# Two attentions in one fused float32 program: values in portions with zero-padded heads, and scores of stacked rows

## The chip, the cores and the metric

One core of one Trainium2 chip runs the whole program in one launch. The metric is the device time of that launch in microseconds (us). Below, TensorE is the matrix engine (its rows say PE, its weight loads PEld), VectorE is DVE, ScalarE is ACT, GpSimd is POOL, and SyncE (SP) issues most of the transfers.

## What is computed

A batch of one with 1024 tokens of width 1024 goes through a short-convolution layer, a stick-breaking attention layer, and a second block with two attentions of its own, a gated merge and a convolved FFN. Everything is float32. The parts that matter here:

```python
def stick_breaking_attention(q, k, v):        # 16 heads of 64
    ...
        z = jnp.einsum('bhqd,bhkd->bhqk', qb, kb) * inv_sqrt_d
    ...
        log_1m_beta = jnp.where(mask, log_beta - z, 0.0)
        suffix = lax.cumsum(log_1m_beta, axis=3, reverse=True) - log_1m_beta
        a = jnp.where(mask, jnp.exp(log_beta + suffix), 0.0)
        outs.append(jnp.einsum('bhqk,bhkd->bhqd', a.astype(vb.dtype), vb))
    ...
    o = o * jax.nn.silu(z)                     # z: the other half of h @ w_qz
    return x + gate[:, None, :] * (o @ w_out)

def _diff_attention(q, k, v, lam, lam_init, subln_g, slopes):   # 4 heads, 2 maps of 64
    ...
        p = jax.nn.softmax(scores, axis=-1)
        a = p[:, :, 0] - lam * p[:, :, 1]
        return jnp.einsum('bhqs,bshe->bqhe', a.astype(v.dtype), v)
    ...
    out = _rmsnorm(out, subln_g) * (1.0 - lam_init)
```

The other attention of the second block is a sliding window of 128 tokens: 8 heads of 64 over 2 key heads, with a sink.

## The kernel before, in words

The program is written out engine by engine; every engine runs its own list, and the lists meet in semaphores that are waited for by name (`at("stick_scan", n)` is the count after which scan n is done). The dense layers are a list of units, products of one 128-column weight tile with the whole activation (line 1362): both operands are split into a high and a low part (`w_hi`, `w_lo`; POOL makes them, lines 1212 and 1217) and three products are added, since TensorE takes its rounded float32 type faster. Each unit's result is read by an engine of its own. In the same way q and k of both attentions lie in DRAM as a high and a low part.

**First attention.** 128 items, one for each head and block of 128 queries, in the order of `STICK_ORDER` (blocks 6, 7, 0, 1, 4, 5, 2, 3 of each head). The steps of a loop over n hold work on different items. TensorE: scores of item n (`scores`, lines 561, 562, and a mask product at 564), the values of the item pair that ends at n - 6 (line 596, on every second step), the transposes of item n - 3 (`turn`, line 576). ScalarE: two sigmoids of the scores (783, 785), then the copies of the transposed block to `a_T` (797). VectorE: a scan over the sigmoid (908), which makes the suffix product. POOL: the factor times that (1264), giving `beta`, four buffers. The lags are the constants `TURN_LAG`, `VALUE_LAG`, `OUT_LAG`. Scores of an item may start when the scan of the former item of the same PSUM banks is done. The values of a head lie in `hin[:, s, 3]` as two packed parts, high and low, so the product's 128 output rows hold both halves of one head: the high part in the head's own 64 rows, the low part in the other 64. To add them, ScalarE copies one half to `s_o` (771), VectorE adds the other (899), and when both heads of a pair are there POOL multiplies by the gate `sz` (1246) and splits the result into `opA` (1250, 1253), the operand of the units of w_out. The value loads (line 1132) stand on SP's queue among the weight loads; `value_in` says when they are in. The parts of v are made behind the units of w_kv: TensorE transposes a unit's output, ScalarE copies it twice (1614), VectorE subtracts (2216), and `v_dram` takes both.

**Second attention.** 16 sliding-window steps (4 blocks of one head each) and then 32 differential steps, one for each head and query block, in the order `DIFF_ORDER` (0, 1, 2, 3, 7, 6, 5, 4). A differential step x has scores of map 1 and map 0 (line 655), VectorE's bias with running maximum (962), ScalarE's exp with sum (828), VectorE's combination of the two maps (997), the turn (675) at lag `DIFF_TURN`, the values (715) at lag `DIFF_VALUE`. Queries and keys have 64 rows a head, so each score is three products of 64 rows (q_hi k_hi, q_lo k_hi, q_hi k_lo), of map 1 on rows 64 to 127 and of map 0 on rows 0 to 63. Four items make a half of a head; behind its values ScalarE squares them, TensorE sums the squares with a product with ones (736), and adds eps times the squared sum of exps by four more products (738). Keys of a head (512 KB, two slots) and its values come in by SP (476, 491), and are waited for whole.

## Time and profile before

| what | value |
|---|---|
| median of 3 runs | 2885.86 us (2883.86 to 2886.23) |
| profiled execution, its own time | 2888.37 us |
| its span | 2886.6 us |
| TensorE busy | 2730.2 us (95%) |
| TensorE weight loads busy | 2273.4 us (79%) |
| VectorE busy | 1331.7 us (46%) |
| ScalarE busy | 876.1 us (30%) |
| POOL busy | 849.6 us (29%) |
| first attention, TensorE's first score product to its last value product | 937.38 to 1245.98 us |
| second attention, TensorE's first score product to its last product | 1725.56 to 1952.62 us |

A busy share is an average over stages with different limits: in the units TensorE is nearly alone, in the attentions four engines take turns in a ring. The span is that of the profiled execution, and the runs' times are of other executions of the same program.

### The profile page before, as it was taken

The page shows a single profiled execution, that of the slowest core. Times are in us where ns is not written, and L with a number is a line of the kernel's source. Part 1 is how long each engine was busy: PE and PEld are TensorE (multiplying, and loading weights), DVE is VectorE, ACT ScalarE, POOL GpSimd, SP SyncE. Part 2 cuts the span into 40 slices and gives each one's busy share as a digit, 9 for nine tenths or more (in the row PEclk, how much of TensorE's full clock was granted, in tenths as well). Part 3 has the DMA queues.
Part 4 walks back from the last instruction along what each step waited for, and adds up shares of the span by engine and source line. Part 5 has one row for each costly group of instructions (what it writes and reads, how often), then busy time and mean ns, then how long its engine had stood idle before and what let it go on. Part 6 is the DMA issues. An engine that isn't in the chain of part 4 may idle for free.

```text
span 2886.6 us, 33895 instructions
## 1 busy us (share of the span) xinstructions
PE 2730.2 (95%) x13015; PEld 2273.4 (79%) x13015; DVE 1331.7 (46%) x1758; ACT 876.1 (30%) x1521; POOL 849.6 (29%) x600
## 2 busy tenths in 40 slices
PE   3899999999899899999999999898999999999998
PEld 2688888788778888877888878777878888888877
DVE  5656665631433666647300007763565423441444
ACT  3300012511411787846111017661252101110111
POOL 1133331022223566620332330113102233233235
PEclk7999999999999999999999999899999999999999
DMA  5244443263456444432443133103231111111113
GB/s 208 88 131 147 135 145 107 81 218 118 168 198 180 114 107 117 110 117 74 148 144 131 51 85 128 45 23 103 73 88 37 51 51 44 52 51 44 52 50 119
DMA packets 302013, 298.19 MB, mean 103 GB/s; under 512 B 15475, under 2 KB 247324, under 8 KB 300572
## 3 DMA queue, kind: packets, MB, share of 16 engines
q1 hardware_dynamic: 292092, 254.61, 29.6%
q10 hardware_dynamic: 9760, 41.42, 3.7%
q8 instruction: 103, 1.69, 0.3%
q14 instruction: 58, 0.48, 0.1%
HBM read 241.98 MB, written 54.00 MB: 103 GB/s over the span
## 4 chain that ended last, share of the span: by engine, by line
PE 80%; DVE 8%; ACT 4%; POOL 3%; DMA 3%; issue 2%; SPq 0%; DVEq 0%; ACTq 0%; POOLq 0%
PE PS L1362 61%; PE PS L1406 4%; PE PS L596 3%; PE PS L576 2%; PE PS L1429 1%; DMA mod_raw<-in_w_ada 1%; PE PS L655 1%; PE PS L715 1%; POOL beta L1264 1%; PE PS L1477 1%; DVE M L1909 1%; PE PS L675 1%; PE PS L637 1%; PE PS L561 1%; DVE w_lo L2009 1%
## 5 line engine op out<-in xcount | busy, mean ns | idle before, releaser
L1362 PE MATMUL PS<-opA,w_hi 128*128 128x512 f32 x4544 | 1417.3, 392 | 20.7 <-POOL w_lo L1217 13.7
L1362 PEld LDWEIGHTS PS<-opA,w_hi 128*128 128x128 f32 x4544 | 858.8, 189 | 201.8 <-POOL w_lo L1217 14.7
L1362 PE MATMUL PS<-opA,w_lo 128*128 128x512 f32 x2272 | 888.6, 391 | 0.0
L1212 POOL CAST w_hi<-w_raw 128x1024 fp32r<-128x1024 f32 (+1 forms) x174 | 181.3, 1042 | 1585.5 <-PE PS L1362 1127.9
L1362 PEld LDWEIGHTS PS<-opA,w_lo 128*128 128x128 f32 x2272 | 429.6, 189 | 89.1 <-issue 0.2
L1217 POOL TENSOR_TENSOR w_lo<-w_raw,w_hi 128x1024 fp32r<-128x1024 f32 (+1 forms) x176 | 425.1, 2415 | 91.5 <-ACT w_hi L1697 77.6
L1362 PE MATMUL PS<-opB,w_hi 128*128 128x512 f32 x1216 | 379.8, 391 | 6.8 <-POOL w_lo L1217 4.4
L1362 PEld LDWEIGHTS PS<-opB,w_hi 128*128 128x128 f32 x1216 | 229.0, 188 | 55.9 <-POOL w_lo L1217 4.8
L1909 DVE SCALAR_TENSOR_TENSOR M<-mod_raw,small,M 128x512 f32<-128x512 f32 x168 | 170.0, 1012 | 171.2 <-DMA mod_raw<-in_w_ada 90.2
L1362 PE MATMUL PS<-opB,w_lo 128*128 128x512 f32 x608 | 237.1, 390 | 0.0
L2192 DVE SCALAR_TENSOR_TENSOR X<-PS,mod,X 128x512 f32<-128x512 f32 x96 | 72.1, 751 | 278.2 <-PE PS L1362 277.5
L908 DVE TENSOR_TENSOR_SCAN M<-PS,beta 128x896 f32<-128x896 f32 (+7 forms) x86 | 115.1, 1353 | 82.9 <-ACT PS L785 82.5
L2138 DVE TENSOR_SCALAR yt<-M,cols 128x512 f32<-128x512 f32 x44 | 65.2, 1482 | 163.4 <-ACT M L1849 160.4
L596 PE MATMUL PS<-a_T,hin 128*128 128x256 f32 (+1 forms) x640 | 139.7, 366 | 0.0
L929 DVE CUSTOM_DVE_ANT_0 prob<-bias,PS 128x256 f32<-128x256 f32 x64 | 23.1, 418 | 252.5 <-PE PS L637 252.5
L1849 ACT ACTIVATE M<-PS 128x512 f32<-128x512 f32 x44 | 26.4, 600 | 353.2 <-PE PS L1362 340.0
L1362 PEld LDWEIGHTS PS<-opB,w_lo 128*128 128x128 f32 x608 | 114.5, 188 | 24.0 <-issue 0.5
L596 PEld LDWEIGHTS PS<-a_T,hin 128*128 128x128 f32 x640 | 117.6, 192 | 15.1
L1264 POOL TENSOR_TENSOR beta<-beta,M 128x895 f32<-128x895 f32 (+7 forms) x86 | 103.1, 1209 | 68.5 <-ACT s_o L771 40.4
L797 ACT ACTIVATE a_T<-PS 128x512 f32<-128x512 f32 (+1 forms) x192 | 87.5, 492 | 52.4 <-PE PS L576 52.4
L2203 DVE SCALAR_TENSOR_TENSOR stage<-PS,stage 128x1024 fp32r<-128x1024 f32 x25 | 30.6, 1225 | 146.4 <-ACT stage L1776 145.9
L2143 DVE SCALAR_TENSOR_TENSOR yt<-M,cols,yt 128x511 f32<-128x511 f32 (+1 forms) x120 | 94.9, 790 | 4.2
(193 smaller groups left out, 3099.2 us busy)
## 6 DMA issues: line engine op xcount, KB each, us to landing
mod_raw<-in_w_ada SPq DMA_DIRECT2D x96, 256.0 KB, 3.0
w_raw<-in_w_up SPq DMA_DIRECT2D x44, 512.0 KB, 3.8
w_raw<-in_w_in SPq DMA_DIRECT2D x34, 512.0 KB, 3.8
w_raw<-in_a_w_in SPq DMA_DIRECT2D x32, 512.0 KB, 4.8
q_dram<-stage ACTq DMA_DIRECT2D x16, 1024.0 KB, 4.0
hin<-q_dram SPq DMA_DIRECT2D x64, 256.0 KB, 6.1
k_dram<-stage ACTq DMA_DIRECT2D x13, 1024.0 KB, 4.1
mod_raw<-in_b_mod_w SPq DMA_DIRECT2D x48, 256.0 KB, 2.9
```

Source lines behind the costliest of these rows:

```text
L596: ins = pe.matmul(dst, v, a_T[g % 2][:, kb, cols_of], start=(kb == 0), stop=(kb == i), skip_group_check=True)
L797: act.activation(dst, src, ACT.Copy).then_inc(act_done, 1)
L908: dve.tensor_tensor_scan(rest[n % FACTORS][:, 0:w][:, ::-1], stick_z(n)[:, ::-1], beta[n % BETAS][:, 0:w][:, ::-1], 1.0, ALU.mult, ALU.byp ...
L1212: pool.tensor_copy(hi, raw).then_inc(pool_done, 1)
L1217: pool.tensor_tensor(lo, raw, hi.bitcast(F32), ALU.subtract).then_inc(pool_done, 1)
L1264: pool.tensor_tensor(b[:, 0:w - 1], b[:, 0:w - 1], rest[n % FACTORS][:, 1:w], ALU.mult).then_inc(pool_done, 1)
L1362: ins = pe.matmul(ps, w[:, k0 + k, :], rhs(part, k0 + k), start=(k == 0 and n == 0), stop=(k == chunks - 1 and n == 2))
L1406: ins = pe.matmul(PS[:, bank(v, hf), :], weight(v, w, k), op_in[:, part, k, hf * HALF:(hf + 1) * HALF], start=(k == 0 and n == 0), stop=(k ...
L1909: dve.scalar_tensor_tensor(out=acc, in0=mod_raw[:, n % 2, :], scalar=c, in1=acc, op0=ALU.mult, op1=ALU.add).then_inc(dve_done, 1)
L2138: dve.tensor_scalar(o, src[:, t0:t0 + HALF], w_of(2), b, ALU.mult, ALU.add).then_inc(dve_done, 1)
L2143: dve.scalar_tensor_tensor(out=o[:, lo:], in0=src[:, t0 + lo - back:t0 + HALF - back], scalar=w_of(tap), in1=o[:, lo:], op0=ALU.mult, op1= ...
L2192: dve.scalar_tensor_tensor(out=X[:, j, t], in0=PS[:, bank(u, hf), :], scalar=mod[:, gate, j:j + 1], in1=X[:, j, t], op0=ALU.mult, op1=ALU. ...
```

## The change

First attention: v is stored once, unsplit (`vplain`), so one copy on ScalarE and no subtraction. Each head's values are loaded to a tile `head_v` of 128 columns per key block of which the other head's 64 are zero (cleared once by POOL). The two heads of a pair then add into the same PSUM banks and rows of their own, and one product by `sz` on VectorE a half is all that is left; ScalarE's copy, VectorE's add and POOL's product by `sz` go. The values of an item pair stand in two portions on two successive steps, `a_T` has four slots, `beta` five, and the lags are 4, 7 and 9.

Second attention: q_hi stands over q_lo in the 128 rows of `opA[:, e, c]`; k_hi is loaded twice, to rows 0 to 63 and 64 to 127, and so is k_lo. Two products of 128 rows make a score, now with q_lo k_lo too. Keys come by map and by halves of 512 columns into three slots. Turn, value and square lags are 2, 4 and 3, pair and probability buffers three, and eps times the squared sum is added to the squares by POOL (`square_eps`) in place of the four products. At the first item of a head the scores of map 0 stand behind the turn.

```diff
-TURN_LAG, VALUE_LAG, OUT_LAG = 3, 6, 7
-BETAS, FACTORS = 4, 3
+TURN_LAG, VALUE_LAG, OUT_LAG = 4, 7, 9
+BETAS, FACTORS = 5, 3
...
-DIFF_TURN, DIFF_VALUE, RMS_LAG = 3, 5, 2
+DIFF_TURN, DIFF_VALUE, RMS_LAG = 2, 4, 3
...
-PAIRS = 4
+PAIRS, PROBS = 3, 3
...
+def key_slot(q):
+
+    return (0, 2, 1)[q % 3]
...
+def diff_map(q):
+
+    return q // 2, 1 - q % 2
...
+        beta = [at(f"beta{i}", AT_X + (28 if i == 4 else 4 * i) * KIB, [T]) for i in range(BETAS)]
+        a_T = [[at("a_T0", AT_M + 18 * KIB, [2, 2 * P])], [at("a_T1", AT_M, [4, 2 * P])],
+               [at("a_T2", AT_A + 28 * KIB, [4, 2 * P]), at("a_T2b", AT_A + 60 * KIB, [2, 2 * P])],
+               [at("a_T3", AT_X + 16 * KIB, [4, 2 * P]), at("a_T3b", AT_X + 20 * KIB, [4, 2 * P])]]
+        head_v = [at(f"head_v{i}", AT_B + (44 + 16 * i) * KIB, [T]) for i in range(2)]
...
         def second_loads(sp):
...
+            def dup(slot, hf, rows, name, cols_of):
+
                 for part in range(2):
...
+                    for place in range(2):
+                        sp.dma_start(keys[slot][part][place * DH:(place + 1) * DH, cols_of].bitcast(F32),
+                                     k2_dram[part, rows, cols_of]).then_inc(k_in[slot][hf], 16)
+                        step(k_in[slot][hf], *name, by=16)
+
+            def diff_keys(q):
+                j, m = diff_map(q)
+                slot = key_slot(q)
...
+                elif q < 3:
+                    sp.wait_ge(pe_done, at("sec_S", 4 * q + 7, 0))
...
+                    former, fm = diff_map(q - 3)
+                    sp.wait_ge(pe_done, at("sec_S", SWA_STEPS + NT * former + NT - 1, fm))
+                rows = slice((1 + j) * P + m * DH, (1 + j) * P + m * DH + DH)
+                for hf in range(2):
+                    dup(slot, hf, rows, ("k_in", "diff", q, hf), slice(hf * HALF, (hf + 1) * HALF))
...
+            diff_keys(1)
+            diff_keys(0)
+            diff_value(0)
+            diff_keys(2)
+            for j in range(1, DIFF_HEADS):
+                diff_value(j)
+                diff_keys(2 * j + 1)
+                if j < DIFF_HEADS - 1:
+                    diff_keys(2 * j + 2)
```

```diff
-            def values(n):
+            def values(n, part):
 
                 h, i = stick_item(n)
-                s, o, g = h % 2, 6 + i // NQ, n // 2
+                s, o = h % 2, 6 + i // NQ
...
+                middle = (i + 1) // 2 - (i > NQ)
+
+                if part == 0:
+                    if n % NT == 1:
+                        pe.wait_ge(value_in[s], at("value_in", h))
+                    if n == 1:
+                        pe.wait_ge(pool_done, at("head_zero"))
+                    pe.wait_ge(act_done, at("stick_hi", STICK_PLACE[n, i // NQ]))
+                    if h >= 2 and h % 2 == 0 and i in (1, NT - 1):
+                        pe.wait_ge(dve_done, at("stick_o", h // 2 - 1, i // NQ))
+                for kb in range(i + 1)[slice(middle, None) if part else slice(0, middle)]:
                     cols_of = slice(P if kb == i else 0, 2 * P)
-                    dst = PS[:, o, q0 + cols_of.start:q0 + 2 * P]
-                    v = hin[:, s, 3, kb * P:(kb + 1) * P].bitcast(F32)
-                    ins = pe.matmul(dst, v, a_T[g % 2][:, kb, cols_of], start=(kb == 0), stop=(kb == i),
+                    ins = pe.matmul(PS[:, o, q0 + cols_of.start:q0 + 2 * P], head_v[s][:, kb * P:(kb + 1) * P],
+                                    a_T[i // 2][kb // NQ][:, kb % NQ, cols_of],
+                                    start=(h % 2 == 0 and i in (1, NT - 1) and kb == 0), stop=(h % 2 == 1 and kb == i),
                                     skip_group_check=True)
-                ins.then_inc(pe_done, 1)
-                step(pe_done, "stick_v", n)
+                if part:
+                    ins.then_inc(pe_done, 1)
+                    step(pe_done, "stick_v", n)
 
...
-                if n >= VALUE_LAG and (n - VALUE_LAG) % 2:
-                    values(n - VALUE_LAG)
+                if n > VALUE_LAG:
+                    part = (n - VALUE_LAG) % 2 == 0
+                    values(n - VALUE_LAG - part, part)
                 if 0 <= n - TURN_LAG < STICK_ITEMS:
                     turn(n - TURN_LAG)
...
-                r = slice(DH * (n % 2), DH * (n % 2) + DH)
...
-                        for y, (pq, pk) in enumerate(((0, 0), (1, 0), (0, 1))):
-                            ins = pe.matmul(dst, opA[r, pq, n // 2, i * P:(i + 1) * P],
-                                            keys[r, n // 4, pk, k0:k0 + width], start=(y == 0), stop=(y == 2))
+                        for part in range(2):
+                            ins = pe.matmul(dst, opA[:, n % 2, n // 2, i * P:(i + 1) * P],
+                                            keys[n // 4][part][:, k0:k0 + width], start=(part == 0), stop=(part == 1))
                 ins.then_inc(pe_done, 1)
                 step(pe_done, "sec_S", x, 0)
...
+                if (x - SWA_STEPS) % NT in (0, NQ):
+                    pe.wait_ge(k_in[key_slot(q)][(x - SWA_STEPS) % NT // NQ], at("k_in", "diff", q, (x - SWA_STEPS) % NT // NQ))
...
-                    for y, (pq, pk) in enumerate(((0, 0), (1, 0), (0, 1))):
+                    for part in range(2):
                         ins = pe.matmul(PS[:, 2 * m + DIFF_BANK[x] + k0 // HALF, 0:width],
-                                        opA[r, pq, 4 + j, i * P:(i + 1) * P],
-                                        keys[r, j % 2, pk, k0:k0 + width], start=(y == 0), stop=(y == 2))
+                                        opA[:, m, 4 + j, i * P:(i + 1) * P],
+                                        keys[key_slot(q)][part][:, k0:k0 + width], start=(part == 0), stop=(part == 1))
...
-                pe.wait_ge(act_done, at("sec_sq", h))
-                pe.wait_ge(pool_done, at("sec_gd", items_of(h)[-1]))
-                pe.matmul(PS[:, turn_bank(c), :], ones[:], d_o[:, 0, :], start=True, stop=False, skip_group_check=True)
-                for b in range(NQ):
-                    ins = pe.matmul(PS[:, turn_bank(c), b * P:(b + 1) * P], eps_of[:], diff_diag[:, NQ * (h % 2) + b, :],
-                                    start=False, stop=True, skip_group_check=True)
-                ins.then_inc(pe_done, 1)
+                pe.wait_ge(pool_done, at("sec_sq_eps", h))
+                pe.matmul(PS[:, turn_bank(c), :], ones[:], d_o[:, 0, :], start=True, stop=True).then_inc(pe_done, 1)
                 step(pe_done, "sec_ss", h)
...
                     diff_scores(t, 1)
-                    diff_scores(t, 0)
+                    if (t - SWA_STEPS) % NT:
+                        diff_scores(t, 0)
...
+                if SWA_STEPS <= t < STEPS and (t - SWA_STEPS) % NT == 0:
+                    diff_scores(t, 0)
...
+            def finish(j, hf, n):
+
+                dve.wait_ge(pe_done, at("stick_v", n))
+                dve.wait_ge(reader(U_BOUT - 1), at("free", U_BOUT - 1))
+                if j:
+                    dve.wait_ge(pool_done, at("stick_out", j - 1, hf))
+                dve.tensor_tensor(s_o[:, hf, :], PS[:, 6 + hf, :], sz[:, j, hf * HALF:(hf + 1) * HALF],
+                                  ALU.mult).then_inc(dve_done, 1)
+                step(dve_done, "stick_o", j, hf)
```

```diff
+                sp.dma_start(head_v[s][:].rearrange(parts_of, b=NT, s=2)[:, :, s, :],
+                             v_dram[h // 2].rearrange(parts_of, b=NT, s=2)[:, :, s, :]).then_inc(value_in[h % 2], 16)
                 step(value_in[h % 2], "value_in", h, by=16)
 
...
+                def square_eps(h):
+
+                    pool.wait_ge(act_done, at("sec_sq", h))
+                    pool.wait_ge(pool_done, now(pool_done))
+                    pool.tensor_tensor(d_o[:, 0, :].rearrange("p (b q) -> p b q", b=NQ),
+                                       d_o[:, 0, :].rearrange("p (b q) -> p b q", b=NQ),
+                                       diff_diag[:, NQ * (h % 2):NQ * (h % 2) + NQ, :], ALU.add).then_inc(pool_done, 1)
+                    step(pool_done, "sec_sq_eps", h)
 
                 def low(h):
```

The first attention on TensorE, head 1, its items 8 to 10 and what stands around them (`hin` holds q and k, `beta` the items' products, `a_T` their transposes, numbers are buffers). Before:

```order
L576 MATMUL PS<-ident,beta_84 128x128 x5
L561 MATMUL PS<-hin 128x512
L562 MATMUL PS<-hin 128x512
L561 MATMUL PS<-hin 128x384
L562 MATMUL PS<-hin 128x384
L564 MATMUL PS<-mask_r,ident_r 128x128
L576 MATMUL PS<-ident,beta_85 128x128 x6
```

and now:

```order
L623 MATMUL PS<-a_T_92,head_v_95 128x256 x3
L601 MATMUL PS<-ident,beta_85 128x128 x5
L586 MATMUL PS<-hin 128x512
L587 MATMUL PS<-hin 128x512
L586 MATMUL PS<-hin 128x512
L587 MATMUL PS<-hin 128x512
L589 MATMUL PS<-mask_r,ident_r 128x128
L623 MATMUL PS<-a_T_92,head_v_95 128x256
L623 MATMUL PS<-a_T3b,head_v_95 128x256 x3
L623 MATMUL PS<-a_T3b,head_v_95 128x128
L601 MATMUL PS<-ident,beta_86 128x128 x6
```

The turns of an item stand one step further from its scores, and each step now has a portion of value products, where they stood in one block on every second step.

The differential steps on TensorE, end of the first half of a head (`aT` are transposes, `vals` values, `prob` exps, `keys` keys). Before:

```order
L675 MATMUL PS<-ident,prob_101 128x128 x7
L655 MATMUL PS<-keys,opA 128x256 x6
L715 MATMUL PS<-aT,vals_98 128x128 x8
L675 MATMUL PS<-ident,prob_103 128x128 x6
L655 MATMUL PS<-keys,opA 128x384 x6
L715 MATMUL PS<-aT,vals_98 128x128 x7
L736 MATMUL PS<-d_o,ones 128x512
L738 MATMUL PS<-diff_diag,eps_of 128x128 x4
L675 MATMUL PS<-ident,vals_97 128x128 x5
L655 MATMUL PS<-keys,opA 128x512 x6
```

and now:

```order
L706 MATMUL PS<-ident,prob_114 128x128 x5
L686 MATMUL PS<-keys_101,opA 128x384
L686 MATMUL PS<-keys_102,opA 128x384
L686 MATMUL PS<-keys_105,opA 128x384
L686 MATMUL PS<-keys_106,opA 128x384
L746 MATMUL PS<-aT,vals_107 128x128 x6
L766 MATMUL PS<-d_o,ones 128x512
L706 MATMUL PS<-ident,prob_115 128x128
L686 MATMUL PS<-keys_101,opA 128x512
L686 MATMUL PS<-keys_102,opA 128x512
```

Six score products of a piece of 512 or fewer keys are four, one product is left of the squares' five, and it stands one item later.

## Rows read from the trace of the kernel before

**Rows 1.** The page, chain that ended last, by engine

```profile
PE 80%; DVE 8%; ACT 4%; POOL 3%; DMA 3%; issue 2%; SPq 0%; DVEq 0%; ACTq 0%; POOLq 0%
```

**Rows 2.** Windows: length, busy us of each engine (instructions), granted clock, DMA share, GB/s

```profile
960.40:1224.70 264.30, 246.14 (x1512) 219.86 (x1512) 165.92 (x141) 213.53 (x421) 174.35 (x153) 0.99 0.43 110
...
1725.50:1744.50 19.00, 18.28 (x84) 17.36 (x84) 11.10 (x54) 11.08 (x40) 0.00 (x0) 0.51 1.03 300
1744.50:1803.00 58.50, 56.35 (x453) 52.02 (x452) 42.54 (x186) 43.57 (x141) 2.14 (x2) 1.00 0.25 89
1803.00:1940.40 137.40, 123.62 (x766) 100.33 (x766) 98.17 (x243) 88.37 (x202) 24.84 (x37) 0.89 0.08 28
```

**Rows 3.** Waits of PE, 960 to 1225: us in total, times, longest

```profile
PE PS L561 <- DVE M L908: 9.3, 10, 0.9
PE PS L561 <- DVE rest L908: 4.7, 5, 0.9
PE PS L576 <- POOL beta L1264: 4.6, 6, 0.8
```

**Rows 4.** Waits of DVE, 1744.5 to 1803

```profile
DVE prob L929 <- PE PS L637: 8.6, 7, 3.2
DVE opA L1004 <- ACT opA L846: 6.0, 6, 1.2
```

**Rows 5.** Waits of DVE, 1803 to 1940.4

```profile
DVE vals L962 <- PE PS L655: 14.7, 7, 3.1
DVE prob L962 <- PE PS L655: 10.3, 14, 2.7
```

**Rows 6.** Groups, 937 to 1250: form, count, busy us, mean ns, idle before

```profile
L1246 POOL TENSOR_TENSOR s_o<-s_o,sz 128x512 f32<-128x512 f32 x16 | 20.5, 1282 | 5.1 <-DVE s_o L899 5.1
...
L771 ACT ACTIVATE s_o<-PS 64x512 f32<-64x512 f32 x32 | 18.9, 592 | 3.4 <-PE PS L596 2.7
```

**Rows 7.** Timeline of PE: start, us, instructions, count (the same twelve products twice)

```profile
1112.21 4.28 PE L596 MATMUL PS<-a_T,hin 128*128 128x256 f32 x12
...
1132.25 2.59 PE L596 MATMUL PS<-a_T,hin 128*128 128x256 f32 x12
```

**Rows 8.** Timeline of PE behind the first attention; in brackets the idle time before

```profile
1252.94 0.50 PE L1362 MATMUL PS<-opA,w_hi 128*128 128x512 f32 x1 [1.91 <-POOL opA L1253]
```

**Rows 9.** Timeline at the first unit of w_qz

```profile
740.03 1.02 ACT L1599 ACTIVATE vt<-PS 128x1024 f32<-128x1024 f32 x1
...
741.31 0.77 PE L1429 MATMUL PS<-opA,w_hi 128*128 128x512 f32 x1 [5.00 <-DVE opA L1988]
```

**Rows 10.** DMA issues: count, KB each, median us to landing

```profile
hin<-v_dram SPq DMA_DIRECT2D x16, 512.0 KB, 4.3
...
vals<-va_dram SPq DMA_DIRECT2D x4, 256.0 KB, 8.6
```

**Rows 11.** Timeline of PE, start of the second attention

```profile
1725.56 8.91 PE L637 MATMUL PS<-keys,opA 64*128 64x128 f32 x42 [7.15 <-DMA opA<-q_dram]
```

**Rows 12.** Timeline of PE in a differential step, and a piece of the chain (units)

```profile
1879.69 0.97 PE L655 MATMUL PS<-keys,opA 64*128 64x512 f32 x6
1880.59 1.60 PE L715 MATMUL PS<-aT,vals 128*128 128x128 f32 x12
...
1699.83 18.60 PE PS L1362 x82
```

**Rows 13.** Timeline, end of the second attention

```profile
1938.80 0.89 DVE L997 SCALAR_TENSOR_TENSOR vals<-vals,small,vals 128x640 f32<-128x640 f32 x1
...
1951.57 1.05 PE L738 MATMUL PS<-diff_diag,eps_of 128*128 128x128 f32 x8
1960.38 0.79 PE L1362 MATMUL PS<-opA,w_hi 128*128 128x512 f32 x1 [7.75 <-POOL w_lo L1217]
```

**Rows 14.** Windows of 3 us: one in the first head, two behind the attention

```profile
1824.00:1827.00 3.00, 3.00 (x12) 2.50 (x12) 2.24 (x6) 1.51 (x3) 0.90 (x1) 0.50 0.00 0
...
1963.00:1966.00 3.00, 3.00 (x8) 2.32 (x8) 0.00 (x0) 0.00 (x0) 0.98 (x1) 0.50 0.97 321
1966.00:1969.00 3.00, 3.00 (x14) 2.43 (x13) 0.00 (x0) 0.00 (x0) 0.00 (x0) 0.99 0.98 335
```

246 lines of the change are left out of this document (88 added, 158 removed).

## The prediction, made before the changed kernel ran

> **What bounds the kernel now.** I read the profile's page first. Its chain is 80% TensorE [rows 1], so a microsecond taken from the other engines is worth something only where TensorE waits for it. The change touches two attentions. Only there, and at the seams around them, can time move; the unit products (line 1362) are untouched. So I cut the trace into windows [rows 2]. The first attention holds TensorE from 937.38 us (its first score product) to 1245.98; its even middle, fourteen heads, is the 264.3 us window, in which TensorE is busy 246.14 at a granted clock of 0.99. The second attention is two stretches: sixteen sliding-window steps (58.5 us) and the differential steps (137.4 us, TensorE busy 123.62, clock 0.89).
>
> In the first attention's middle TensorE waits 18.6 us in all: score products for the scan (9.3 + 4.7) and turns for the beta product on POOL (4.6) [rows 3]. These are one thing: with a short item next, the ring of score, two sigmoids, scan, beta product, turn comes round too late. ScalarE is in that ring and is 81% busy (213.53 of 264.3).
>
> In the second attention I read VectorE's waits, since scores, running maximum, exp and turn form a ring there too. In the sliding-window part VectorE waits for score products 8.6 us, 3.2 of it once at the start [rows 4]. In the differential part it waits for them 14.7 + 10.3 = 25.0 us [rows 5]. So neither TensorE nor VectorE is full there: each idles while the other holds the ring.
>
> **First attention, part by part.** *Removed:* ScalarE's half-output copies, 32 of 592 ns = 18.9 us, and POOL's products by sz, 16 of 1282 ns = 20.5 us [rows 6]. VectorE's 32 adds become 16 products by sz of 512 columns, half as many. Turn, value and output lags go from 3, 6, 7 to 4, 7, 9 steps with a fifth beta buffer, and the value products of an item pair come in two portions on two successive steps, where they now stand in one block of up to 16 (2.59 us for 12 [rows 7]). *Not changed:* the number of products. Values still take one 128x256 product per key block. So TensorE's busy 246.14 stays, and the gain can come from waits alone. A turn a step later has one more step of TensorE work (about 2.2 us, 264.3 / 112 items = 2.36 less the waits) to hide the scan and beta product; the longest wait of the 21 is 0.9. ScalarE has 18.9 us less to do in the ring. I take all 18.6 as gone. The 12 value products at 1112.21 took 4.28 us where the same twelve took 2.59 twenty us later [rows 7]: the clock fell once, after two waits of 0.93 and 0.78. With no waits I take that 1.7 as gone. **A: -20.3.** Bounds: 0 and -20.3, and I come near the far end because the cover (2.2 us) is over twice the longest wait.
>
> *Start.* Turns begin one step later and values too, and TensorE has less to do meanwhile, and the last items drain one step longer. One step costs 2.36 at most and 0 at least: **B: +2**. *Seam to w_out of that layer.* After the attention TensorE stops 1.91 us for POOL's second opA split [rows 8]; POOL's product by sz (1282 ns) ahead of it is gone and the whole is shorter: **C: -1.9**; bounds 0 and -1.9.
>
> *Seam between w_kv and w_qz.* VectorE's value split (two subtracts per value block) goes, and ScalarE's two copies become one. TensorE waits 5.00 us until 741.31, and ScalarE's value copy from PSUM still stands at 740.03 to 741.05 [rows 9]. That copy is not removed, only two of 1.31 before it become one, so the start moves little. **D: -1** with the smaller stalls behind. Bounds 0 and -2.
>
> *Value loads.* Per head 256 KB in runs of 64 numbers instead of 512 KB in long ones. The nearest rows are the sliding-window values, the same pattern at 8.6 us to landing, against 4.3 for today's value loads [rows 10]. It is issued when the values of the head before last are done and is wanted about a head (18.9 us, 264.3 / 14) later. Cost 0, hidden by that head; without that cover it would be 4.3 a head. The memsets of the zero columns stand in POOL's idle stretch before 937.
>
> **Second attention.** *Start.* The first 42 sliding-window score products take 8.91 us, 0.212 each, at half clock [rows 11]. Three products of 64 rows become two of 128, so 28: 14 x 0.212 = 3.0. The queries now come as 64-row pieces and I have no row for these, so I keep only **E: -1.8**; bounds 0 and -3.0. *Sliding-window steps.* Of the 8.6 us of waits [rows 4], the 3.2 at the start belongs to E's low clock. Of the other 5.4 I take 3.3, about three fifths: beside them VectorE waits 6.0 for ScalarE's output [rows 4], which the change leaves alone, and the steps bound there stay as they are. **F: -3.3**; bounds 0 and -5.4.
>
> *Differential steps.* Here the change says "two products instead of three", and the rows say otherwise. Six 64-row products of 512 columns, three on rows 0 to 63 and three on rows 64 to 127, run from 1879.69 to the next product at 1880.59: 0.90 us, 0.15 each. A full 128-row product of 512 columns costs 18.60 / 82 = 0.227 [rows 12]; four are 0.91. So on items up to 512 keys the two products cost what the three did. The Trainium skill, TensorEngine Tiling (Array Packing), section Tiling Modes, says of this that tiles on different rows work independently, with a speedup of up to 2, so that the change gives something up: by the full factor six products would cost 0.68 where four stacked ones cost 0.91, 36 such groups in the four heads would lose 8 us, and the sum would be -36. The trace bears out a factor of 1.5 (0.15 against 0.227), by which the two forms tie.
>
> What is gained is elsewhere: the four eps products behind each half's sum of squares go (8 records, 1.05 us [rows 13]; eight halves: 8.4 us of TensorE), the turn comes a step sooner, and only each head's key half that is needed is waited for. POOL adds one 128x512 sum per half (1282 ns by the same form in [rows 6]); the lag of the root-mean-square goes from two to three steps and covers it. Of the 25.0 us I keep half as still there: at head ends one item's scores must wait for values, turn and squares in TensorE's own order, four or five waits of nearly 3 (the longest is 3.1), and the clock is half for a stretch after 1819 [rows 14]. Keys: the load of each head's second map now waits for the last item of the map three back, and lands 4.3 to 8.6 us later (the two rows of [rows 10]); TensorE has one step of 4.3 us (137.4 / 32) plus that step's first scores and turns to do, and the second map's scores are put behind the turns for that. I cost it at nothing; without cover it is up to 2 a head at three heads. **G: -13**; bounds 0 and -25. *Last head.* From the last combine, at 1939.69, to the first branch product at 1960.38 is 20.7 us [rows 13]. A value lag one shorter, no eps products and earlier turns leave about 16: turn 0.6, values 2.6, squares' sum and its copy, then the same chain to w_lo. **H: -4.7**; bounds 0 and -8.
>
> **Sum.** -20.3 + 2 - 1.9 - 1 - 1.8 - 3.3 - 13 - 4.7 = **-44.0**. The profiled execution took 2888.37 us (span 2886.6), 2.5 above the median of 2885.86; so the changed one is 2844.4 profiled, and 2842 as a median.
>
> **Rivals.**
> *B1: the first attention keeps its waits.* ScalarE is 81% busy and its order changes; the fifth beta buffer may bring nothing if the scan itself is the bound (VectorE 165.92 of 264.3 speaks against it). Then A gives 5 rather than 20.3: -28.7, 2857 us. 0.10.
> *C1: the second attention gives nothing.* A shorter turn lag takes cover away: scores, maximum, exp and combination must be through within two steps, not three, and with three pairs of buffers rather than four VectorE waits for the turns of three steps ago, with that item's maximum and the combination behind it in its queue and ScalarE's exp behind those. Then E to H fall away: -44 + 22.8 = -21.2, **2865 us**. 0.10.
> *D1: the clock comes back sooner.* After the gap behind this attention, where the next products are of 128 rows, it was at half from the start at 1960.38 until 1966 only (0.50, then 0.99 [rows 14]), against the 19 us from 1725.5 (0.51 [rows 2]) with products of 64 rows. If stacked products do the same, 13 us fewer at half clock at the start and some 10 in the first head: the ratio of the two rows of [rows 7] is 1.65, so each gives back 0.4: 23 x 0.4 = 9 to 11, total about -55, 2831 us. 0.12.
> *E1: slower, by the clock.* The clock stays at its lower level through the whole second attention, since the ring's gaps now fall differently. The differential part's clock of 0.89 means about 30 of its 137.4 us at half; its TensorE work at full clock is then 123.62 - 30 + 30 / 1.65 = 112, less 8.4 for eps = 103, times 1.65 = 171: +33. The sliding-window steps: 56.35 less 54 products of about 0.13 = 49, times 1.65 = 81: +22. With E to H gone and A to D kept: -21.2 + 55 = **+34, 2920 us**. It makes the whole slower once about 40% of the second attention stands at low clock (21.2 / 55). Against it: in [rows 2] the clock came back each time, and the stacked products fill all rows. 0.05.
> That the change doesn't do what it says I see at one place only, the three-to-two products above, and the sum has it.
>
> **How the numbers follow.** Forecast 0.60 at 2842, B1 0.10, C1 0.10, D1 0.12, E1 0.05, and 0.03 for B1 and C1 together (-6, about no change). Upward the range takes in B1 and C1: 2866. Downward D1's 2831 and then G at its bound of -25 instead of -13, of which I take 11: 2820. **2820 to 2866**; E1, the joint case and the ends of the forecast are outside. A measurement can tell about 0.2%, 5.8 us. Slower by more: E1, 0.05. Within it: the joint case, 0.03. Faster: the rest, 0.92.
>
> **What would show it.** In the first attention: no waits of L561's line on the scan, and a distance of 17.5 to 17.9 us between heads in place of 18.9; clock 1.00. The add and the copies gone from ScalarE, whose busy falls by about 19. In the second: VectorE's waits for score products about 12 us in place of 25.0, and score products of 512 columns at 0.227, in pairs, with no saving of time per narrow item; the last combine to first branch product about 16 us. The prediction is wrong if the first attention still takes over 300 us, or if the second attention shows less than 10 us gained by its windows, or if the granted clock there lies under 0.8.

## The result and the profile after

| | before | changed |
|---|---|---|
| median | 2884.86 us (4 runs, 2880.42 to 2886.23) | 2833.49 us (4 runs, 2832.38 to 2836.87) |
| ratio, with 95% interval | | 0.9827 [0.9809, 0.9844] |
| span of the profiled execution | 2886.6 us | 2830.6 us |
| forecast | | 2842 us, range 2820 to 2866 |

The kernel is 51.4 us faster, 7.4 more than the -44.0 of the sum. Cut at the same places, the two profiled executions (2886.6 - 2830.6 = 56.0) say where. Every number of the table is a difference of starts on TensorE's timeline; the last combine is VectorE's, by its end. (The 1245.98 us given above as the end of before's first attention is the start of the first product of the units behind it, as in the table.)

| stretch | before | changed | difference | terms of the sum |
|---|---|---|---|---|
| start to the first transpose of v | 659.06 | 652.68 | -6.4 | none |
| to the first score product of the first attention | 278.32 | 277.94 | -0.4 | D -1 |
| first attention to the first product of the units behind it | 308.60 | 280.72 | -27.9 | A, B -18.3 |
| of it fourteen heads | 264.26 | 238.27 | -26.0 | A -20.3 |
| to the second attention | 479.58 | 477.86 | -1.7 | C -1.9 |
| its start to the first differential score | 74.40 | 64.72 | -9.7 | E, F -5.1 |
| to the end of the last combine (the differential steps) | 139.73 | 128.14 | -11.6 | G -13 |
| to the first branch product (the drain) | 20.69 | 21.06 | +0.4 | H -4.7 |
| to the end | 926.22 | 927.48 | +1.3 | none |

The first line is not the change's. In the fourteen kernels profiled for this study, on which TensorE has the same instructions in the opening, the second modulation sum (a group of small products with `ones`) starts anywhere from 136.98 to 142.24 us, and the sum after it from 184.07 to 190.89; before is at the late end (190.56), the changed kernel at the early one (184.16). So some 50 of the 56 are the change's, which is what the medians say.

The same fourteen show how closely the other lines can be read, since many of them share the instructions of a stretch. From the first transpose to the first attention takes 271.5 to 278.3 us, and from the first attention to the second 476.7 to 479.9, with and without the change, so D and C are not read from these two lines. Six kernels (the changed one, e2, e5, e6, e9, e11) have the changed second attention to the instruction: 64.7 to 65.2 us up to the first differential score, and 128.1 to 130.3 in the differential steps, where the changed kernel is the lowest. The three with the former one (before, e1, e3) have 73.4 to 74.6 and 138.9 to 141.2. A difference of 1 us is read in neither stretch. The fourteen heads are steadier: the eight kernels that share them have 238.28 us each.

The page and the waits of TensorE, 930 to 1225 us, changed kernel (us in total, times, longest):

```profile
PE 84%; DVE 8%; ACT 3%; DMA 3%; issue 1%; POOL 1%; SPq 0%; DVEq 0%; ACTq 0%; POOLq 0%
```

```profile
PE PS L586 <- DVE M L923: 3.5, 2, 2.8
PE PS L586 <- POOL w_hi L1229: 1.3, 1, 1.3
PE PS L601 <- ACT a_T L814: 0.9, 1, 0.9
PE PS L586 <- DVE rest L923: 0.2, 1, 0.2
```

All of these are ahead of the fourteen heads, in the fill. TensorE is now 84% of the chain [rows 1], and the three rows of [rows 3] have no counterpart in the steady heads. The windows, in the form of [rows 2]: the fourteen heads, then the start of the second attention, the rest of its sliding-window steps, and the differential steps.

```profile
952.37:1190.64 238.27, 238.27 (x1515) 216.04 (x1513) 158.59 (x127) 203.85 (x392) 157.81 (x139) 1.00 0.47 108
...
1689.00:1701.00 12.00, 9.23 (x47) 8.58 (x48) 8.20 (x40) 6.64 (x25) 0.00 (x0) 0.68 1.12 223
1701.00:1754.00 53.00, 47.81 (x406) 45.70 (x404) 43.45 (x195) 43.94 (x145) 2.14 (x2) 1.00 0.74 170
1754.00:1882.00 128.00, 100.49 (x649) 84.58 (x647) 99.02 (x249) 90.64 (x212) 33.42 (x43) 0.97 0.20 59
```

In the first row TensorE is busy for the whole of the window at full clock: the first attention is now bound by TensorE alone. In the second attention the clock is back after some 12 us where it took 19 before, and is 0.97 in the differential steps in place of 0.89, while TensorE is busy 100.49 of 128 and VectorE 99.02: there the ring is the bound. VectorE's waits there, in the form of [rows 5], for scores and for turns:

```profile
DVE prob L977 <- PE PS L686: 5.3, 5, 1.7
DVE prob L977 <- PE PS L706: 2.7, 9, 1.3
DVE vals L977 <- PE PS L686: 2.6, 3, 1.2
...
DVE vals L977 <- PE PS L706: 2.4, 2, 2.2
```

Those for scores are 7.9 us in place of 25.0; those for turns are 5.1 where they were 0.5. ScalarE has 204 of 238 us to do in the first attention where it had 213.5 of 264.

### The profile page after: what moved, and what is told of

Its sections match the earlier page's. It is cut to its first block, busy times and chain, and to the rows that moved or that the text cites. A ratio compares the mean times of both kernels' runs of the same rounds, so it can differ in the third digit from the quotient of the medians.

```text
span 2830.6 us, 33366 instructions
## 1 busy us (share of the span) xinstructions
PE 2677.3 (95%) x12783; PEld 2235.0 (79%) x12783; DVE 1310.7 (46%) x1726; ACT 860.8 (30%) x1481; POOL 844.2 (30%) x594
## 4 chain that ended last, share of the span: by engine, by line
PE 84%; DVE 8%; ACT 3%; DMA 3%; issue 1%; POOL 1%; SPq 0%; DVEq 0%; ACTq 0%; POOLq 0%
PE PS L1393 63%; PE PS L623 5%; PE PS L1437 4%; PE PS L601 2%; PE PS L1460 2%; DMA mod_raw<-in_w_ada 1%; PE PS L587 1%; PE PS L586 1%; PE PS L1508 1%; DVE M L1923 1%; PE PS L746 1%; PE PS L706 1%; DVE w_lo L2021 1%; DVE prob L977 1%; PE PS L686 1%
## 5 line engine op out<-in xcount | busy, mean ns | idle before, releaser
L623 PE MATMUL PS<-a_T,head_v 128*128 128x256 f32 x448 | 116.7, 378 | 0.0
L1993 DVE TENSOR_TENSOR xn<-X,M 128x512 f32<-128x512 f32 x80 | 57.4, 717 | 86.0 <-PE PS L1393 81.5
L800 ACT ACTIVATE beta<-PS 128x896 f32<-128x896 f32 (+7 forms) x128 | 83.4, 652 | 22.1 <-PE PS L589 20.4
```

What stands on the lines that cost most here:

```text
L623: ins = pe.matmul(PS[:, o, q0 + cols_of.start:q0 + 2 * P], head_v[s][:, kb * P:(kb + 1) * P], a_T[i // 2][kb // NQ][:, kb % NQ, cols_of], ...
L800: act.activation(beta[n % BETAS][:, 0:w], z, ACT.Sigmoid).then_inc(act_done, 1)
```

## The experiments

They were measured in three groups, each with its own runs of the kernel before: e1 to e4 with a median of 2882.13 us, e5 to e8 with 2883.23, e9 to e12 with 2879.98. The changed kernel, 2833.49, was measured beside 2884.86. So medians of different groups can differ by some 5 us for no reason of the kernels, and where a difference is as small as that it is taken from the traces' stretches instead.

### The two parts alone

e1 has the constants `TURN_LAG` to `BETAS`, the value tiles, portions and finishes of the first attention; e2 has the rest of the diff.

```diff
 # e1
+TURN_LAG, VALUE_LAG, OUT_LAG = 4, 7, 9
+BETAS, FACTORS = 5, 3
 DIFF_TURN, DIFF_VALUE, RMS_LAG = 3, 5, 2
...
 # e2
 TURN_LAG, VALUE_LAG, OUT_LAG = 3, 6, 7
 BETAS, FACTORS = 4, 3
+DIFF_TURN, DIFF_VALUE, RMS_LAG = 2, 4, 3
+PAIRS, PROBS = 3, 3
```

> Only the first attention's part of the change. Theory 1 (the two parts act alone, each in its own window): the first attention, 308.6 us from its first score product to the first product of the units behind it, falls by 28.0 as in the changed kernel, and the seams around it by 2; the whole by about 30. Rival (part of the 51 us is chance in the first 140 us, where the changed kernel's profiled execution was already 6.3 us ahead without a changed instruction on TensorE): the time falls by 30 too, but the position at 140 us stands as in before. Forecast as the prediction had it: -21.

> Only the second attention's part. Theory 1: 9.7 us less up to the first differential score, 11.6 less in the differential steps, nothing at the drain: about -21 in all, so that e1 and e2 add up to the whole change. Rival (the parts interact, by the clock or by ScalarE): the sum of the two differs from the whole by more than 5 us.

e1: 2849.92 us, ratio 0.9896 [0.9873, 0.992], -32.2. e2: 2862.28 us, ratio 0.9936 [0.9915, 0.9957], -19.9. Together -52.1, the whole change -51.4: the parts act alone, as far as intervals of 6 to 7 us to either side can tell. In e1 the first attention takes 280.79 us and the second attention's stretches are those of before (74.59, 138.93, 20.70); in e2 the first takes 308.64 and the second's are the changed kernel's (65.16, 128.95, 21.06). The rival of e1 holds for the profiled executions: e1's second modulation sum starts at 140.43 and e2's at 142.24, like before's 140.65 and not like the changed kernel's 137.08.

### What took the first attention's waits away

e3 is the kernel before with one more step of turn lag and the fifth beta buffer:

```diff
-TURN_LAG, VALUE_LAG, OUT_LAG = 3, 6, 7
-BETAS, FACTORS = 4, 3
+TURN_LAG, VALUE_LAG, OUT_LAG = 4, 6, 7
+BETAS, FACTORS = 5, 3
```

> The kernel before with a turn lag of 4 in place of 3 and the fifth beta buffer, nothing else: ScalarE's copies, POOL's products by sz and the value blocks stay. If the lag is what took TensorE's waits away (18.6 us of 21 waits, and some 0.27 more at each that the waits' rows do not show), the first attention's heads come to about 17.1 us and the time falls by 22 to 26. If the waits go because the value products come in portions or because ScalarE and POOL have less to do, the heads stay near 18.8 us and the time falls by under 8.

2894.72 us, ratio 1.0048 [1.0031, 1.0066]: slower by 12.6. Both of my theories missed it. Heads are 19.62 us, where they were 18.88 on the mean, and the first attention takes 320.84 us in place of 308.60. TensorE's waits, 955 to 1230 us:

```profile
PE PS L576 <- ACT a_T L797: 18.4, 42, 0.6
PE PS L561 <- DVE M L908: 5.5, 9, 0.6
PE PS L561 <- DVE rest L908: 3.0, 5, 0.6
```

The waits for POOL's beta of [rows 3] are gone, and those for the scan fall from 14.0 to 8.5, but TensorE now waits 18.4 us for ScalarE to copy the transposes out of PSUM. A later turn moves the wait from the ring to ScalarE, in whose queue those copies stand behind two sigmoids, with half-output copies between. That it is the place in the queue is read from the kernel's order and not shown by itself.

Then three kernels that leave one or two of the three ingredients out of the changed kernel: portions (e5), the lag (e6), both (e9).

```diff
 # e5, e9
-                middle = (i + 1) // 2 - (i > NQ)
+                middle = 0
...
 # e6, e9
-TURN_LAG, VALUE_LAG, OUT_LAG = 4, 7, 9
+TURN_LAG, VALUE_LAG, OUT_LAG = 3, 7, 9
```

> The changed kernel with the values of an item pair in one block on the second of the two steps, as it stood before; lags, buffers and zero-padded heads as changed. The turn lag alone made the heads 19.6 us (TensorE waited 18.4 us for ScalarE's copies of the transposed blocks). Theory 2 (portions are what keeps TensorE fed: with a block on every second step the steps without values are too short for ScalarE's two sigmoids and copies): heads of 17.02 us go back to 18.3 or more, the time is 18 us or more above the changed kernel's. Rival (the copies and products taken off ScalarE and POOL did it): heads stay under 17.4 us, the time is within 5 us.

> The changed kernel with a turn lag of 3 in place of 4. If the lag is needed, TensorE waits for the scan and for beta again behind short items (before: 18.6 us in 21 waits): heads of 17.8 us or more, +11 us or more. If the portions alone did it, heads stay at 17.0 to 17.2 us and the time is within 3 us of the changed kernel's, with one step less at the drain.

> The changed kernel with a turn lag of 3 and the values in one block, so of the first attention's part only the zero-padded heads and what they take off ScalarE and POOL are left. Heads so far: before 18.83 us, lag alone 19.62, changed 17.02, without portions 17.50, without the lag 17.41. Theory 5 (what is taken off ScalarE and POOL does most): heads of 17.7 to 18.0 us, the time 11 to 16 us above the changed kernel's. Rival (the padded heads help only together with lag or portions): heads of 18.3 or more, 20 us or more above.

| kernel | turn lag | portions | padded heads (ScalarE and POOL relieved) | us per head | median, us |
|---|---|---|---|---|---|
| before | 3 | no | no | 18.82 | 2884.86 |
| e3 | 4 | no | no | 19.62 | 2894.72 |
| e9 | 3 | no | yes | 17.94 | 2849.09 |
| e5 | 4 | no | yes | 17.50 | 2844.54 |
| e6 | 3 | yes | yes | 17.42 | 2841.34 |
| changed | 4 | yes | yes | 17.02 | 2833.49 |

(A head is the distance from one head's first short item to the next. Where heads alternate between two lengths, as 18.34 and 19.30 do in before, it is the mean of such a pair; the 18.88 above is the mean of before's fourteen, one of which holds the clock's fall. e5: ratio 0.9873 [0.9857, 0.9889]; e6: 0.9857 [0.984, 0.9875]; e9: 0.9889 [0.9871, 0.9907].) Neither of the two sides that I had written for e5 and e6 is right as it stands: the heads lie between, at 17.5 and 17.4. For e9 theory 5 holds: 17.94 us a head, 15.6 above the changed kernel. The padded heads with what they take off the other engines are the largest single step, 0.9 us a head by itself and 2.1 with the lag (19.62 to 17.50). The lag is worth 0.4 with them and costs 0.8 without them. Portions are worth 0.5.

One thing stays together in all of these: e5, e6 and e9 also keep the changed kernel's later values and its four slots of `a_T`, and no kernel has those beside the old heads. The slots are not what helps: in before and in e3 every wait of ScalarE in front of such a copy (39.4 and 41.7 us between 960 and 1190) is for the transposes, none for the value products that free a slot. That the values of another item pair now stand beside each score is not told apart from the relief, nor is ScalarE's relief from POOL's and VectorE's. TensorE's waits in e9, 957 to 1200 us, show what is left without lag and portions:

```profile
PE PS L601 <- ACT PS L802: 8.3, 6, 1.4
PE PS L601 <- ACT a_T3b L814: 2.8, 7, 0.4
```

(L802 is the second sigmoid, L814 the copy of the transposes; the file of e9 has the changed kernel's lines.)

### Stacked rows

e4 is the changed kernel with the second attention's queries, keys and score products as before; lags, three buffers and POOL's eps stay. The keys' halves and the later scores of map 0 go with the stacking, so they are undone with it.

```diff
-                    for part in range(2):
+                    for y, (pq, pk) in enumerate(((0, 0), (1, 0), (0, 1))):
...
-                                        opA[:, m, 4 + j, i * P:(i + 1) * P],
-                                        keys[key_slot(q)][part][:, k0:k0 + width], start=(part == 0), stop=(part == 1))
+                                        opA[r, pq, 4 + j, i * P:(i + 1) * P],
+                                        keys[r, j % 2, pk, k0:k0 + width], start=(y == 0), stop=(y == 2))
```

> The changed kernel with the second attention's scores as before: three products of 64 rows, queries and keys loaded as before; lags, three buffers, and eps by POOL as changed. Theory from the prediction (the two forms tie on items of up to 512 keys): the differential steps are within 2 us of the changed kernel's 128.1, the sliding-window part loses 3 to 5 us (its products of one head have no second row group beside them: 42 in 8.91 against 28 in 5.71). Rival (stacking is where the second attention's gain comes from, by fewer low-clock microseconds or by shorter scores): the time is 12 or more above the changed kernel's.

2847.39 us, ratio 0.988 [0.9851, 0.9909]: 13.9 above the changed kernel (17.6 by the two stretches that follow). The rival holds and my tie falls. The sliding-window stretch is 73.68 us (changed 64.72, before 74.40), the differential one 136.76 (128.14, 139.73). So of the 9.7 and 11.6 us of gain, stacking, with the loads that go with it, makes 9.0 and 8.6 by these three executions; lags, buffers and eps make 0.7, which is within the scatter, and 3.0. With the ranges above, stacking's part of the differential steps is 6.5 to 8.6. The timeline of TensorE in e4, a differential item of four key blocks and then items of eight, seven and six, at full clock; behind it the weight loads of the items of eight and seven:

```profile
1844.61 0.98 PE L670 MATMUL PS<-keys,opA 64*128 64x512 f32 x6
1845.53 1.38 PE L730 MATMUL PS<-aT,vals 128*128 128x128 f32 x10
...
1847.06 2.24 PE L670 MATMUL PS<-keys,opA 64*128 64x512 f32 x12
1849.22 0.49 PE L730 MATMUL PS<-aT,vals 128*128 128x128 f32 x2
...
1850.48 2.90 PE L670 MATMUL PS<-keys,opA 64*128 64x512 f32 x12 [0.45 <-DVE small L958]
1853.31 0.71 PE L730 MATMUL PS<-aT,vals 128*128 128x128 f32 x4
...
1854.46 2.58 PE L670 MATMUL PS<-keys,opA 64*128 64x512 f32 x12
1856.97 0.94 PE L730 MATMUL PS<-aT,vals 128*128 128x128 f32 x6
```

```profile
1847.05 1.81 PEld L670 LDWEIGHTS PS<-keys,opA 64*128 64x128 f32 x12 [0.17 <-issue]
1850.48 1.16 PEld L670 LDWEIGHTS PS<-keys,opA 64*128 64x128 f32 x6 [0.68 <-DVE small L958]
1851.89 1.17 PEld L670 LDWEIGHTS PS<-keys,opA 64*128 64x128 f32 x6 [0.24 <-DVE small L958]
```

Six products of the item of four are 0.92 us (1844.61 to 1845.53), as in [rows 12], and the twelve of 512 columns of the item of eight 2.16, 0.18 each: they overlap, and no wait stands between the two maps. The item of seven has six of 512 and six of 384, fewer columns, and takes 2.83 us; less the 0.24 of the wait in its middle that is 2.59. By an estimate from the 0.227 of [rows 12], twelve products without overlap would take 2.38 (6 x 0.227 and 6 x 0.170, by columns). The two maps wait for VectorE one after the other, so that map 1's six have nothing beside them on the other half of the rows: six weight loads take 1.16 us and 1.17, where the item of eight has twelve in 1.81. An item of four and the items of seven and six in the changed kernel (TensorE):

```profile
1796.55 1.17 PE L686 MATMUL PS<-keys,opA 128*128 128x512 f32 x4
1797.56 1.28 PE L746 MATMUL PS<-aT,vals 128*128 128x128 f32 x10
...
1802.62 1.08 PE L686 MATMUL PS<-keys,opA 128*128 128x512 f32 x4 [0.57 <-DVE small L977]
1804.02 1.09 PE L686 MATMUL PS<-keys,opA 128*128 128x512 f32 x4 [0.32 <-DVE small L977]
...
1806.60 0.96 PE L686 MATMUL PS<-keys,opA 128*128 128x512 f32 x4 [0.61 <-DVE small L977]
1807.87 0.97 PE L686 MATMUL PS<-keys,opA 128*128 128x512 f32 x4 [0.31 <-DVE small L977]
1808.68 0.83 PE L746 MATMUL PS<-aT,vals 128*128 128x128 f32 x6
```

The items of seven and six take 1.08 + 0.93 = 2.01 and 0.96 + 0.81 = 1.77 us of TensorE in place of 2.59 and 2.51, four products a map where six were. On the item of four key blocks, where the two forms were said to tie, the changed kernel's four products take 1.01 us (1796.55 to 1797.56), not less than e4's 0.92, and on the item of eight 2.10 where e4 has 2.16. In the sliding-window steps one head uses one half of the rows only, so nothing overlaps at all. The first row below is e4's, the second the changed kernel's, for steps of the same shape:

```profile
1718.84 1.99 PE L652 MATMUL PS<-keys,opA 64*128 64x128 f32 x15
```

```profile
1703.07 1.41 PE L667 MATMUL PS<-keys,opA 128*128 128x128 f32 x10
```

From the first of these products to the next instruction's start it is 1.92 us and 1.24: a third less, 0.7 us a step.

The clock goes with it. Start, sliding-window and differential steps in e4's windows, the form of [rows 2]:

```profile
1691.00:1711.00 20.00, 18.75 (x93) 17.81 (x94) 11.10 (x54) 11.21 (x40) 0.00 (x0) 0.55 1.07 313
1711.00:1765.30 54.30, 53.54 (x433) 49.63 (x431) 40.80 (x181) 40.62 (x129) 2.14 (x2) 1.00 0.24 84
1765.30:1902.00 136.70, 123.11 (x744) 99.06 (x744) 100.69 (x248) 91.22 (x212) 34.02 (x43) 0.88 0.09 32
```

0.88 of 136.7 us is about 33 us at half clock, 0.97 of 128 is 8. e7 asks whether count of products or clock did it: three products of 128 rows in the differential scores. Its scores are not the reference's there, since the low key part is multiplied twice.

```diff
-                    for part in range(2):
+                    for part in (0, 1, 2):
...
+                                        keys[key_slot(q)][min(part, 1)][:, k0:k0 + width], start=(part == 0), stop=(part == 2))
```

> The changed kernel with a third product of 128 rows in every differential score (k_lo once more, so the scores of the differential heads are not the reference's), the sliding-window part as changed. It tells the clock from the count of products in the 8.6 us that unstacking cost in the differential steps. Theory 3 (the clock: with all 128 rows in use it comes back sooner; unstacked it was at half for about 33 of 136.7 us, changed for about 8 of 128): the granted clock of the differential steps stays at 0.95 or more, and they take 2 to 6 us longer than 128.1 for 36 x 2 more products of 0.227 = 16 us of TensorE's, of which VectorE's ring hides most. Rival (the count of products decides it, the clock follows from waits): the steps take 8 us or more longer, or the clock falls below 0.92.

2837.83 us, ratio 0.9848 [0.9832, 0.9864]: theory 3 holds. The differential stretch is 132.76 us, +4.6, at a clock of 0.96:

```profile
1753.40:1886.20 132.80, 116.92 (x745) 102.12 (x745) 99.10 (x249) 91.16 (x212) 33.44 (x43) 0.96 0.19 57
```

TensorE is busy 116.92 us, 16.4 more than changed, of which the ring hides 12. So unstacking costs 8.6 and a third product of full rows 4.6, at the clock of the stacked form. That the other 4.0 is the clock fits these two rows; it is not shown by itself, since e4 also loads its keys otherwise. One pair shows how little low clock can cost here: e5's second attention is the changed kernel's to the instruction, yet its differential steps had a granted clock of 0.92 in place of 0.97, some 21 us at half clock in place of 8, and took 130.28 us in place of 128.14.

### Eps and the end of the second attention

e8 adds eps by four products as before; e10 by one product with `ones` over a half's four blocks, put ahead of the sum of squares.

```diff
 # e10, in rms; POOL's square_eps goes
+                pe.wait_ge(pool_done, at("sec_gd", items_of(h)[-1]))
+                pe.matmul(PS[:, turn_bank(c), :].rearrange("p (b q) -> p b q", b=NQ), ones[:],
+                          diff_diag[:, NQ * (h % 2):NQ * (h % 2) + NQ, :], start=True, stop=False)
+                pe.wait_ge(act_done, at("sec_sq", h))
+                pe.matmul(PS[:, turn_bank(c), :], ones[:], d_o[:, 0, :], start=False, stop=True).then_inc(pe_done, 1)
```

> The changed kernel with eps added by four products on TensorE as before, not by POOL on the squares. Theory 4 (at the drain POOL's add stands in the chain: TensorE waited 4.5 us for it, and the last combine to the first branch product took 21.1 us where I had forecast 16): the drain falls by 1 to 2 us since the products are 0.5 to 1 us longer than no products but the add (1.26) and the low split in front of it (1.26) leave the chain; the differential steps lose 0 to 3 us; the whole is within 2 us of the changed kernel's. Rival (the eps products were a large part of the gain in the steps, 8.4 us of TensorE): +5 us or more.

> The changed kernel with eps added by one product with ones over the four blocks of a half (512 columns), put ahead of the sum of squares in the same bank, and no add on POOL. In the drain the product is done while the squares are not there yet, and POOL's add (1.26 us) and the split it queues behind (1.26) leave the chain: last combine to first branch product 18 to 19.5 us in place of 21.06. In the differential steps one more product a half (0.9 us x 8), hidden or up to 3 us. The whole: -3 to +1 us. Rival (the chain at the drain is bound by something else, as in the run with four products: 20.9): no change of the drain.

e8: 2833.00 us (ratio 0.983 [0.9816, 0.9845]), differential stretch 129.07, drain 20.94. e10: 2831.90 us (0.9829 [0.9809, 0.9848]), 129.03 and 18.64. The rival of e8 falls, and so does its theory's 1 to 2 us at the drain. Both stretches, 129.07 and 129.03, lie inside the 128.1 to 130.3 of kernels that share the changed form, so eps by POOL is worth nothing that can be told from chance in the steps, where step G had named 8.4 us of TensorE's time for it. At the end it costs as much as the four products did (21.06 against 20.94), and one product in its place saves 2.4 us, as e10 expected. The end of the changed kernel, TensorE and then POOL:

```profile
1886.66 1.02 PE L766 MATMUL PS<-d_o,ones 128*128 128x512 f32 x2
1887.52 1.28 PE L746 MATMUL PS<-aT,vals 128*128 128x128 f32 x10
1893.32 2.04 PE L766 MATMUL PS<-d_o,ones 128*128 128x512 f32 x2 [4.52 <-POOL d_o L1349]
1903.12 0.79 PE L1393 MATMUL PS<-opA,w_hi 128*128 128x512 f32 x1 [7.76 <-POOL w_lo L1234]
```

```profile
1890.51 1.26 POOL L1359 TENSOR_TENSOR opA<-d_o,opA 128x512 fp32r<-128x512 f32 x1 [4.54 <-ACT opA L883]
1891.91 1.26 POOL L1349 TENSOR_TENSOR d_o<-d_o,diff_diag 128x512 f32<-128x512 f32 x1
1898.19 1.26 POOL L1359 TENSOR_TENSOR opA<-d_o,opA 128x512 fp32r<-128x512 f32 x1 [5.01 <-ACT opA L883]
1899.61 1.04 POOL L1229 CAST w_hi<-w_raw 128x1024 fp32r<-128x1024 f32 x1 [0.16 <-POOL opA L1359]
1900.73 2.34 POOL L1234 TENSOR_TENSOR w_lo<-w_raw,w_hi 128x1024 fp32r<-128x1024 f32 x1
```

The last squares are there at 1890.9 (ScalarE). POOL has first to split the half before (until 1891.8) and then to add eps (until 1893.2); TensorE waits 4.52 us, and does the sum at half clock behind that gap, 2.04 us (granted clock 0.50), where the same two records took 1.02 at 1886.66. And from 1893.2 to 1898.2 POOL does nothing, then takes 3.4 us for a weight tile that has nothing to do with the attention. e11 puts that tile's split in the hole, and lets TensorE do the unit's sliding-window half, which reads nothing of the last heads, before it waits; e12 is e10 and e11 together.

```diff
 # e11, POOL's loop
+                    h = half_at(t, RMS_LAG + 1)
+                    if h == 2 * DIFF_HEADS - 1:
+                        pool.wait_ge(pe_done, at("sec_T", last_piece(STEPS - 2)))
+                        split(U_BRANCH)
+                    if h is not None:
+                        low(h)
...
 # e11, TensorE, branch units
-                pe.wait_ge(pool_done, at("sec_out", 2 * DIFF_HEADS - 1))
                 for hf in range(2):
                     rhs = lambda part, k: opA[:, part, k, hf * HALF:(hf + 1) * HALF]
                     product(PS[:, 2 * s + hf, :], w_hi[:, s], w_lo[:, s], rhs, 4, 0, ("unit_a", u, hf))
+                for hf in range(2):
+                    rhs = lambda part, k: opA[:, part, k, hf * HALF:(hf + 1) * HALF]
+                    pe.wait_ge(pool_done, at("sec_out", 2 * DIFF_HEADS - 2 + hf))
                     product(PS[:, 4 + 2 * s + hf, :], w_hi[:, s], w_lo[:, s], rhs, 4, 4, ("unit", u, hf))
```

> The changed kernel with POOL's split of the first branch tile put ahead of its last opA split, and TensorE's products of the sliding-window half of that unit (24 products, 5.4 us at full clock) ahead of the wait for the last differential half. Theory 6 (the end of the second attention is a chain through all engines of which 3.4 us are w_hi and w_lo and 5.4 us are products that wait for nothing there): the first branch product starts about 5 us or more earlier, and the time falls by 6 to 10 us against the changed kernel's 2833.5. Rival (TensorE makes up for nothing because the second unit's tile or the clock, at half behind the gap, bounds the branch): under 3 us.

> Both of the former together: eps by one product and the end rearranged. If they act on different links of the chain: -8 to -12 us against the changed kernel, 2822 to 2826 us. If they hide each other: no better than the rearranged end alone.

e11: **2823.81 us** (2822.82 to 2825.40), ratio 0.98 [0.978, 0.9821] to the kernel before. That is 9.7 under the changed kernel's median, but 56.2 under its own group's before where the changed kernel was 51.4 under its own, so the medians leave 5 to 10 us. The trace says 6.3 (the drain below). e12: 2825.93 us (2822.78 to 2835.01), ratio 0.9813 [0.9789, 0.9837]. TensorE and POOL in e11:

```profile
1891.53 1.36 PE L766 MATMUL PS<-d_o,ones 128*128 128x512 f32 x2 [4.52 <-POOL d_o L1349]
1895.06 0.79 PE L1395 MATMUL PS<-opA,w_hi 128*128 128x512 f32 x1 [2.18 <-POOL w_lo L1234]
```

```profile
1892.66 2.35 POOL L1234 TENSOR_TENSOR w_lo<-w_raw,w_hi 128x1024 fp32r<-128x1024 f32 x1
1895.71 1.28 POOL L1359 TENSOR_TENSOR opA<-d_o,opA 128x512 fp32r<-128x512 f32 x1 [0.70 <-ACT opA L883]
```

The drain is 14.79 us in place of 21.06, and 14.26 in e12: with the tile ahead of the last split, the chain through squares and eps is hidden behind TensorE's 24 products, so e10's 2.4 us are not to be had a second time. That theory of e12 (they hide each other) is the right one: the drain is only 0.5 us shorter than e11's, and the medians do not differ beyond their scatter. e11 is faster than the kernel before and the changed one.

## Why the prediction was right, and where its steps were not

The time, 2833.49, lies in the range and 8.5 us below the forecast. The signs of six of the eight terms held; the reasons of A and G did not. That the sum came so near is in part luck: A, B, E and F together gained 14 us more than the sum had, and G and H 6.5 less.

**A (-20.3, measured -26.0).** Right that all of TensorE's waits go and that the cover is enough. Mis-sized: the rows of waits gave 18.6 us and the clock 1.7; 5.7 more came. Over two steady heads, from start to next start and without the idle time, a product of the turns takes 0.101 us in before and 0.091 in the changed kernel, a mask product 0.093 and 0.072, while the score products differ by under 0.002 and the value products are 0.003 longer in the changed one. In before a turn or mask product just ahead of a wait takes 0.27 us where its fellows take 0.08 to 0.10, which no row of waits counts. 5.7 over 21 waits is 0.27 each, the products just behind a wait included. And the reason that I gave, the later turn, is by itself harmful (e3). The padded heads with their relief, which the step named second, carry it. The relief of ScalarE is itself smaller than the 18.9 counted for it: the lengths of its instructions in the first attention add up to 281.6 us in before and 262.3 now, but its busy time falls only from 245.11 to 234.97, since neighbouring instructions overlap in the rows. I had said that lag, portions and relief go together, but took the cover of a step as sufficient without asking whether ScalarE could copy the transposes in time.

**B (+2, measured -1.9).** The fill's heads became shorter with the others (17.99 to 16.75 for the first), which is more than the extra step.

**C and D (-1.9, -1)** hold by TensorE's waits at the two seams, where the stretches scatter too much. The 1.91 us behind the first attention are gone; e2, without this part of the change, still has 1.89. At w_qz the waits of 5.00 and 0.35 us are one of 4.29, 1.1 less, now for POOL's w_lo tile; the copy's ending no longer matters.

**E and F (-5.1, measured -9.7).** F took three fifths of VectorE's waits as gone. All went but 2.2 of the 8.6 [rows 4], and the clock came back 7 us sooner. The third of the score products saved is a real third here, since one head's rows have no partner.

**G (-13, measured -11.6): right size, wrong reason.** "So on items up to 512 keys the two products cost what the three did": true, measured again in e4, and near true for the item of eight blocks (2.10 against 2.16 us). The step failed in going from there to the whole: where the two maps are released one after the other, and in the sliding-window steps, the three cost full price. The eps products and the earlier turn, to which I gave the gain, are worth 3.0 with the buffers, and that the size came out near is luck. VectorE's waits for score products in the steps are 7.9 us, where I had said 12, and yet the steps gained no more than the sum: VectorE now waits 5.1 us for turns, where it waited 0.5. The Trainium skill, TensorEngine Tiling (Array Packing), section Tiling Modes, says that tiles on different rows can load weights and multiply in parallel. The trace agrees where both maps are free at once (0.15 us a product against 0.227), and shows nothing of it where one waits until the other's products are done (0.194 us a weight load against 0.151). I had weighed that rule with the one row where it held best.

**H (-4.7, measured +0.4).** The step said that no eps products and a shorter lag shorten the end. The last squares do come sooner, 8.9 us behind the last combine where it was 10.9. But the step left out that POOL's add takes the products' place in the chain, behind another split in POOL's queue (2.4 us, as e10 shows), and that the sum then runs at half clock behind the longer gap. "The lag of the root-mean-square goes from two to three steps and covers it" is true where steps follow, and false for the last half, where none does.

**The rivals.** B1 and C1 did not occur, and neither did E1: the clock in the differential steps was 0.97 where E1 needed it low throughout. D1 (the clock comes back sooner, 0.12) did, in the start of the second attention (12 us of window at 0.68 against 19 at 0.51) and in the differential steps (about 8 us of low clock in place of 30), and it is a part of what the sum lacked; how many us of the 9.7 and 11.6 it gave is not shown. Of the signs that I had named, the heads (17.5 to 17.9 us; measured 17.02) and the drain (about 16; 21.06) came out otherwise.
